# Two product forms in the feed-forwards' gate and up stage, and another order of the late projections in the first block

## What is computed

```python
t_mat = triangular_solve(a_mat, eye)     # 32 matrices of 64x64: the substitution
za, qb, zb, ga, gb = split(h @ w_rest)   # the late projections: 3584 columns

def _swiglu(h, w_gate, w_up, w_down):    # 4 times: 2 layers x 2
    return (jax.nn.silu(h @ w_gate) * (h @ w_up)) @ w_down
```

## Time and profile before

| | |
|---|---|
| Median of 3 runs | 1714.55 us (1713.25 to 1716.82) |
| The profiled execution | 1717.84 us, of it 1715.9 us span |
| TensorE busy | 1566.3 us, 91% of the span |
| VectorE busy | 978.8 us, 57% |
| ScalarE busy | 604.1 us, 35% |
| GpSimd busy | 205.0 us, 12% |
| Chain that ended last | PE 78%, DVE 10%, ACT 6%, DMA 2%, issue 2% |
| Gate and up products | 3 x 1408 matmuls of 256 columns |

### The profile page before, as it was taken

How to read it: one execution, slowest core, us unless ns; L and a number is a source line. 1 busy time by engine, 2 the same in 40 slices (tenths; PEclk the granted TensorE clock), 3 DMA queues, 4 the chain that set the end, 5 groups by cost and what they waited for, 6 DMA issues and landing times.

```text
span 1715.9 us, 21713 instructions
## 1 busy us (share of the span) xinstructions
PE 1566.3 (91%) x8944; PEld 1231.6 (72%) x8944; DVE 978.8 (57%) x1482; ACT 604.1 (35%) x945; POOL 205.0 (12%) x205
## 2 busy tenths in 40 slices
PE   7997869888889999899989998799998999989998
PEld 2646446545469997785459996699977865489986
DVE  0477775844147777355337776467776453275444
ACT  2425121132034443262234443444433531153442
POOL 0021142000001110043001110011100240001100
PEclk9998969998989999999989999999999999989999
DMA  9444323133347869332338887377976323457551
GB/s 343 141 128 146 98 75 123 59 126 122 123 146 264 282 229 359 130 123 92 106 111 269 265 288 276 116 247 257 311 281 217 123 74 111 147 178 227 185 172 49
DMA packets 192105, 305.44 MB, mean 178 GB/s; under 512 B 6139, under 2 KB 116487, under 8 KB 191879
## 3 DMA queue, kind: packets, MB, share of 16 engines
q1 hardware_dynamic: 189088, 299.45, 51.5%
q10 hardware_dynamic: 2919, 4.61, 0.7%
HBM read 302.99 MB, written 1.05 MB: 177 GB/s over the span
## 4 chain that ended last, share of the span: by engine, by line
PE 78%; DVE 10%; ACT 6%; DMA 2%; issue 2%; POOL 1%; ACTq 0%; DVEq 0%; POOLq 0%
PE ps L380 76%; DVE accs L521 2%; PE ps L383 2%; DVE wlo L1955 1%; ACT whi L1913 1%; DMA ring<-in_w_mod_dram 1%; DMA ring<-in_ffn_w_down_dram 1%; DVE arena L1212 1%; DVE arena L1209 1%; DVE H L1802 1%; DVE H L1736 1%; ACT arena L1447 0%; DVE misc L1514 0%; ACT hhi L1918 0%; DMA ctab<-in_consts_dram 0%
## 5 line engine op out<-in xcount | busy, mean ns | idle before, releaser
L1955 DVE TENSOR_TENSOR wlo<-ring,whi 128x1024 fp32r<-128x1024 f32 x264 | 322.5, 1225 | 221.9 <-ACT whi L1913 215.1
L380 PE MATMUL ps<-hhi,whi 128*128 128x256 f32 x1408 | 406.5, 289 | 20.9 <-DVE hlo L1961 14.9
L380 PE MATMUL ps<-hlo,whi 128*128 128x256 f32 x1408 | 402.0, 286 | 0.0
L380 PE MATMUL ps<-hhi,wlo 128*128 128x256 f32 x1408 | 401.9, 285 | 0.0
L1913 ACT ACTIVATE whi<-ring 128x1024 fp32r<-128x1024 f32 x264 | 274.8, 1055 | 314.4 <-PE ps L380 281.1
L380 PEld LDWEIGHTS ps<-hhi,whi 128*128 128x128 f32 x1408 | 274.4, 195 | 23.4 <-DVE hlo L1961 21.7
L380 PE MATMUL ps<-ring,H 128*128 128x512 f32 (+1 forms) x608 | 266.7, 589 | 13.5 <-ACT arena L1007 6.1
L380 PEld LDWEIGHTS ps<-hlo,whi 128*128 128x128 f32 x1408 | 274.2, 195 | 1.7 <-issue 1.7
L380 PEld LDWEIGHTS ps<-hhi,wlo 128*128 128x128 f32 x1408 | 274.0, 195 | 0.0
L380 PEld LDWEIGHTS ps<-ring,H 128*128 128x128 f32 x608 | 114.6, 195 | 134.1 <-issue 116.8
L521 DVE SCALAR_TENSOR_TENSOR accs<-ring,misc,accs 128x512 f32<-128x512 f32 x266 | 201.3, 757 | 2.7
(11 more groups left out here) (289 smaller groups left out, 1429.5 us busy)
## 6 DMA issues: line engine op xcount, KB each, us to landing
ring<-in_w_mod_dram SPq DMA_DIRECT2D x84, 1024.0 KB, 6.3
ring<-in_w_in_dram SPq DMA_DIRECT2D x48, 1024.0 KB, 5.1
ring<-in_ffn_w_gate_dram SPq DMA_DIRECT2D x44, 1024.0 KB, 7.3
ring<-in_ffn_w_up_dram SPq DMA_DIRECT2D x44, 1024.0 KB, 5.5
ring<-in_ffn_w_down_dram SPq DMA_DIRECT2D x44, 1024.0 KB, 6.5
ring<-in_w_out_dram SPq DMA_DIRECT2D x12, 1024.0 KB, 4.9
gates<-in_b_mod_dram SPq DMA_DIRECT2D x7, 512.0 KB, 7.3
ring<-in_w_proj_a_dram SPq DMA_DIRECT2D x2, 1024.0 KB, 6.1
```

The costliest lines, as they stand in the source:

```text
L380: return self.e.matmul(o, lhsT, rhs, start=start, stop=stop)
L1955: v.done(v.e.tensor_tensor(lo, M.slot(key)[:, r0:r0 + rn, :], plain(hi), ALU.subtract), ("split", l, sub, n), *([M.freed(key)] if ends els ...
```

## The change

In the feed-forwards HHI and HLO become the two halves of one tensor HH. The products hi x hi and hi x lo of a contraction tile become one product of 512 columns with `whi` as the stationary operand: columns 0 to 255 get hi x hi, columns 256 to 511 get hi x lo. The product lo x hi (256 columns) is added to the first half. Gate and up of a tile get a PSUM bank each; the pool `"ga"` now has six banks, so that a tile takes the two banks that the tile three before it held. The tail of a tile becomes longer: ScalarE copies the second halves of both banks (512 elements) into SG, VectorE adds the first halves of both (512 elements) and frees the banks, then ScalarE takes silu of the sum in SG (256), VectorE multiplies (256, both operands in SG), and `ahi` and `alo` follow as before. The copies, the sums, the silus and the products of the two tiles of a pair are each done for both before the next kind. TensorE reports the first tile of a pair when it is done, half a piece before the second. In `split_all` the tail now comes before the split of the pair's fourth piece is handed on, and not behind it. The column counts stay: 768 for each contraction tile and hidden tile, in two products and not three.

In the first block the order of the late projections is 1, 2, 0, 3, 4 and not 1, 2, 3, 4, 0. Before the wait for the substitution TensorE does 14 ticks of them and not 8 (tiles 1, 2, 0 and half of 3), and the tick behind y6 goes. Tile 0 uses banks 6 and 7. ScalarE takes tile 2 out before it waits for the substitution, and tile 0 after the first copies of y5. The weights of 1, 2, 0, 3 are fetched in a row, then two chunks of w_mod, then those of 4.

```diff
...
 NS = 5
-POOLS = {... "ga": (0, 1, 2, 3),
+POOLS = {... "ga": range(6),
          "down": (2, 3, 4, 5), "chain": (2, 3, 4, 5), "proj": (0, 1), "rec": (2, 3), "sd": (4, 5, 6), "dbo": (7,), "outx": (2, 3, 0, 1), "ds": (4, 5, 6, 7), "turnf": (6, 7, 0, 1), "turnx": (6, 7, 4, 5)}
...
         with nc.sbuf_tensor("arena", [128, self.AR], f32) as arena:
             self.arena = arena
         self.WHI, self.WLO = self.sbr("whi", [128, 4, 1024]), self.sbr("wlo", [128, 4, 1024])
-        self.HHI, self.HLO = self.sbr("hhi", [128, 8, 256]), self.sbr("hlo", [128, 8, 256])
+        self.HH = self.sbr("hh", [128, 2, 8, 256])
+        self.HHI, self.HLO = self.HH[:, 0, :, :], self.HH[:, 1, :, :]
         self.AHI, self.ALO = self.sbr("ahi", [128, 22, 256]), self.sbr("alo", [128, 22, 256])
         self.slots, self.banks, self.at = {}, {}, 0
         self.misc_at = self.bc_at = 0
...
 def pe_rest(pe, part):
     for n in part:
-        yield from pe_tok(pe, ("rest", n), 256, "rest")
+        yield from pe_tok(pe, ("rest", n), 256, "mods" if n == 0 else "rest")
 def act_rest(a, n, *after):
...
 def sp_delta(sp, mods):
-    run(sp_rest(sp, [1, 2]))
-    tick(mods, 8)
-    rest = sp_rest(sp, [3, 4, 0])
-    tick(rest, 1)
-    tick(mods, 8)
-    run(rest)
+    run(sp_rest(sp, [1, 2, 0, 3]))
+    tick(mods, 16)
+    run(sp_rest(sp, [4]))
 def pe_blocks(pe, key, col, pairs, width):
...
 def pe_delta(pe, mods):
     M = pe.M
-    fill = pe_rest(pe, [1, 2, 3, 4, 0])
+    fill = pe_rest(pe, [1, 2, 0, 3, 4])
     pe.sums = "mods"
     pe_tokens(pe, 1, M.VF, ("silu", 7))
     for blk in range(2):
...
         pe_decay(pe, n)
         if n in (5, 7):
             tick(fill, 1)
-    tick(fill, 6)
+    tick(fill, 12)
     lo, up = slice(0, 64), slice(64, 128)
     l5 = [(slice(0, 32), slice(32, 64)), (slice(64, 96), slice(96, 128))]
     B, F, G, Y5, Y6 = M.B, M.F, M.G, M.Y5, M.Y6
...
             pe.wait_ge(("x5 out", s, 0), ("x5 out", s, 1))
             pairs = [(at % 8, B[lo, m, up], (G[lo, m, :] if d == 0 else F[lo, m, lo])) for m, at in mats(s, d)]
             pe_blocks(pe, ("y6", s, d), 64, pairs, 64)
-    tick(fill, 1)
     for s in range(2):
         for d in range(2):
             pe.wait_ge(("y6 out", s, d))
...
     act_tokens(a, 1, M.VTOK)
     act_decays(a, 4, 10)
     act_rest(a, 1, ("dd read", 9), ("dd read", 7))
+    act_rest(a, 2)
     a.wait_ge(("tx",), ("clear",))
     for b in range(4):
         a.done(a.e.activation(blocks(M.F, b, 0, b), turned(M.TX, b, 0), ACT.Copy), ("blocks",))
-    act_rest(a, 2)
     for s in range(2):
         key = ("y5", s, 0)
         a.wait_ge(key)
         a.done(a.e.activation(M.Y5[32:64, s * 16:s * 16 + 16, :], M.ps(key)[32:64, :].rearrange("p (m c) -> p m c", c=32), ACT.Copy),
                ("y5 out", s, 0), ("free", key))
+    act_rest(a, 0, ("blocks",))
     for s in range(2):
         key, m0, m1 = ("x5", s, 0), slice(s * 16, s * 16 + 8), slice(s * 16 + 8, s * 16 + 16)
         a.wait_ge(key)
...
         a.wait_ge(key)
         a.done(a.e.activation(M.F[0:64, s * 16:s * 16 + 8, 64:128], M.ps(key)[0:64, :].rearrange("p (m c) -> p m c", c=64), ACT.Copy),
                ("x6 out", s), ("free", key))
-    for n in (3, 4, 0):
+    for n in (3, 4):
         act_rest(a, n, ("x6 out", 1), ("blocks",))
...
 def spare(M):
-    return [M.H[:, k, 256:512] for k in range(8)]
+    return [M.H[:, 2 * i:2 * i + 2, 256:512] for i in range(3)]
 def piece(M, i, n):
...
     ps_ = pieces(l, sub)
     for f in range(0, 22, 2):
         for q in range(4):
+            if q == 3:
+                yield f
             if f < 20:
                 emit(ps_[4 * (f // 2) + 4 + q])
             elif q < 3:
                 emit(ps_[44 + q])
             if work is not None:
                 tick(work, beside(f, q))
-        yield f
     emit(ps_[47])
     for kt in range(19):
         yield ("down", kt)
...
 def act_ffn(a, l, sub):
     M = a.M
-    SG = spare(M)[0:3]
+    SG = spare(M)
     def emit(p):
         n, key, r0, rn, wd_, _ = p
...
     for p in first[1:]:
         emit(p)
     for f in split_all(a, l, sub, emit, None):
-        for j in range(2 if isinstance(f, int) else 0):
-            i, key = (f + j) % 3, ("gu", l, sub, f + j)
-            a.wait_ge(("gu", l, sub, f), ("alo", l, sub, f + j - 3))
-            a.done(a.e.activation(SG[i], M.ps(key)[:, 0:256], ACT.Silu), ("silu", l, sub, f + j))
+        pair = range(f, f + 2) if isinstance(f, int) else ()
+        for x in pair:
+            key = ("gu", l, sub, x)
+            b = M.banks[key, 0]
+            a.wait_ge(key, ("alo", l, sub, x - 3))
+            a.done(a.e.activation(SG[x % 3], M.psum[:, b:b + 2, 256:512], ACT.Copy), ("copied", l, sub, x))
+        for x in pair:
+            a.wait_ge(("summed", l, sub, x))
+            a.done(a.e.activation(SG[x % 3][:, 0, :], SG[x % 3][:, 0, :], ACT.Silu), ("silu", l, sub, x))
+        for j, x in enumerate(pair):
+            i = x % 3
             a.wait_ge(("act", l, sub, f + j))
-            a.done(a.e.activation(M.AHI[:, f + j, :], SG[i], ACT.Copy), ("ahi", l, sub, f + j))
+            a.done(a.e.activation(M.AHI[:, f + j, :], SG[i][:, 0, :], ACT.Copy), ("ahi", l, sub, f + j))
 def pool_ffn(g, l, sub):
     M = g.M
-    SG = spare(M)[0:3]
+    SG = spare(M)
     for f in range(22):
         g.wait_ge(("ahi", l, sub, f))
-        g.op(g.e.tensor_tensor(M.ALO[:, f, :], SG[f % 3], plain(M.AHI[:, f, :]), ALU.subtract), ("alo", l, sub, f))
+        g.op(g.e.tensor_tensor(M.ALO[:, f, :], SG[f % 3][:, 0, :], plain(M.AHI[:, f, :]), ALU.subtract), ("alo", l, sub, f))
 def v_ffn(v, l, sub, work):
     M = v.M
-    SG = spare(M)[0:3]
+    SG = spare(M)
     def emit(p):
         n, key, r0, rn, wd_, ends = p
...
     for f in split_all(v, l, sub, emit, work):
         for j in range(2 if isinstance(f, int) else 0):
             i, key = (f + j) % 3, ("gu", l, sub, f + j)
+            b = M.banks[key, 0]
+            v.wait_ge(("copied", l, sub, f + j))
+            v.done(v.e.tensor_tensor(SG[i], SG[i], M.psum[:, b:b + 2, 0:256], ALU.add), ("summed", l, sub, f + j),
+                   ("free", (key, 0)), ("free", (key, 1)))
+        for j in range(2 if isinstance(f, int) else 0):
+            i = (f + j) % 3
             v.wait_ge(("silu", l, sub, f + j))
-            v.done(v.e.tensor_tensor(SG[i], SG[i], M.ps(key)[:, 256:512], ALU.mult), ("act", l, sub, f + j), ("free", key))
+            v.done(v.e.tensor_tensor(SG[i][:, 0, :], SG[i][:, 0, :], SG[i][:, 1, :], ALU.mult), ("act", l, sub, f + j))
 def pe_ffn(pe, l, sub, work):
     M = pe.M
     for f in range(0, 22, 2):
-        bs = [pe.bank(("gu", l, sub, f + j), "ga") for j in range(2)]
         for q in range(4):
             n = 2 * f + q
             hi, lo = piece(M, n, 256)
-            o0, k0 = 256 * (q // 2), 4 * (q % 2)
+            k0 = 4 * (q % 2)
             pe.wait_ge(("split", l, sub, n), ("hlo", l, sub, q % 2))
             for j in range(2):
-                c = slice(j * 128, j * 128 + 128)
-                for kt in range(4):
-                    ins = pe.mm3(bs[j][:, o0:o0 + 256], (hi[:, kt, c], lo[:, kt, c]), (M.HHI[:, k0 + kt, :], M.HLO[:, k0 + kt, :]),
-                                 k0 + kt == 0, k0 + kt == 7)
-            pe.done(ins, ("staged", l, sub, n), *([("gu", l, sub, f)] if q == 3 else []))
+                c, key = slice(j * 128, j * 128 + 128), ("gu", l, sub, f + j)
+                if q == 0:
+                    for i in range(2):
+                        pe.bank((key, i), "ga")
+                b = M.ps((key, q // 2))
+                for kt in range(k0, k0 + 4):
+                    low = lambda: pe.mm(b[:, 0:256], lo[:, kt - k0, c], M.HHI[:, kt, :], False, False)
+                    if kt:
+                        low()
+                    ins = pe.mm(b, hi[:, kt - k0, c], M.HH[:, :, kt, :], kt == 0, kt == 7)
+                    if kt == 0:
+                        low()
+                if q == 3 and j == 0:
+                    pe.done(ins, key)
+            pe.done(ins, ("staged", l, sub, n), *([key] if q == 3 else []))
             tick(work, beside(f, q))
     bs = [[pe.bank(("d", l, sub, blk, hf), "down") for hf in range(2)] for blk in range(2)]
     for k0 in range(19):
```

2 lines of the change are left out of this document (1 added, 1 removed).

## The result

| | before | changed |
|---|---|---|
| Median of 19 runs each | 1716.07 us (1712.61 to 1720.95) | 1706.57 us (1699.70 to 1715.10) |
| Ratio | | 0.9948, 95% interval 0.9935 to 0.9961 |
| The profiled execution, its span | 1717.84 us, 1715.9 us | 1711.62 us, 1709.6 us |

The change makes the kernel 8.9 us faster (0.0052 x 1716), not 26.7. The direction was right; the time lies above the forecast's range of 1672 to 1704.

What follows compares the result with a forecast made beforehand. TensorE sets the pace in gate and up, VectorE close behind; in the first block TensorE stands still for VectorE's substitution. Feed-forwards -11.7 and first block -15 make -26.7, from 1714.55 to 1687.8 us; range 1672 to 1704.

Steps and rivals of the forecast that it cites:

- The wide product: Gate and up stages: 0.347 us a contraction tile, not 0.360; 18.7 us less over four stages if TensorE alone decides.
- The tail: First three gate and up stages: VectorE's longer tail makes TensorE wait, leaving 2.5 us less per stage and not 4.7.
- the wait at its end: End of gate and up: the down stage waits for banks the last tiles hold, 1.6 to 2.2 us in first and third.
- VectorE is there about 3 us earlier: First and third down stages: VectorE's steps come about 3 us earlier, so the new bank wait ahead of them counts nothing.
- the ring: Weight slots: up's slot is freed 3 us later; 1 us added to each of the first three stages for a late slot.
- The fourth feed-forward: Last feed-forward, with modulation steps in its first four pairs only: 5.9 us less, 1.7 of it from the down-stage wait.
- The first block: Six more ticks fill TensorE's 21.1 us gap; the fence comes at 311 and not 326.6, -15 us, between -10 and -19.
- the wait at tile 4: First block, behind x6: TensorE waits for ScalarE to take tile 3 out of banks 0 and 1; 3.5 us lost.
- 128 records at the 0.0206 us that the warm ones of x5 take: First block, y5 behind the substitution: it finds a warm clock and takes 2.6 us, not 6.4.
- Everything behind the fence moves with it.: After the first block: the whole gain to the fence is kept, with 0 us change from there to the first feed-forward.
- The slower side: Gate and up: the tail lengthens VectorE's pair past TensorE's old pace, bank waits in each pair's first piece; 1755 us, chance 0.09.
- the wide product saves nothing: Gate and up: two runs of 256 columns cost as much as two products, pace stays 11.52 us; 1696.6 us, chance 0.09.

Runs made afterwards that it cites:

- ffn_only: The changed kernel with the first block's stage as before, so only the feed-forwards are changed; 1712.22 us, 0.9984 of the kernel before.
- delta_only: The kernel before with only the first block's new order of late projections, feed-forwards as before; 1711.26 us, 0.9977 of the kernel before.
- one_step: The changed kernel with one modulation step at every piece, never two; 1687.58 us, 0.9835 of the kernel before.
- before_one_step: The kernel before with one modulation step at every piece, never two; 1693.16 us, 0.9894 of the kernel before.
- one_step_banks: The changed kernel with one modulation step at every piece and tile 4 of the late projections in banks 6 and 7; 1680.73 us, 0.9811 of the kernel before.
- old_tail: The changed kernel with the tail moved back behind the split of the pair's fourth piece; 1837.7 us, 1.0730 of the kernel before.

## Why the prediction was wrong

By the medians of `ffn_only` and `delta_only` the feed-forwards gave 2.7 us of the 11.7 forecast and the first block 4.0 of 15. Both halves failed, by 9 and by 11 us.

**The wide product** (forecast 18.7 us in all, 0.347 us a contraction tile). Mis-sized: the runs show 0.352 and 0.360, which saves 1408 x 0.008 = 11 us. The step that failed read the extra of 0.0133 us off two streams of one width each, in two stages, and took it as a property of each product. The wide product of this stage has about 0.019 (0.232 less 0.2133), even in a row of its own width. Neither the layout nor the order of widths nor the load of the other engines explains the 0.005; what does stays open. Per product taken out, the saving is 8 ns by the timeline, 5.5 by the spans. The Trainium skill, "TensorE: Matmul & The Clock Gate", section "Back-to-back issue gap", has about 2.5 ns for the fixed part of an isolated warm product, by which an estimate for 1408 would be 3.5 us. The measurement lies between that and my 13.3, and it decides. The same section of the Trainium skill also says that the spacing in a stream is set by the load of the stationary operand and the product together, which speaks against adding up one width's spacing and another's as I did.

**The tail** (forecast 2.5 us less for a stage, the wait at its end apart). The mechanism is right: waits of 1.33 and 0.41 us for the sum, and one of 0.06, stand in the first piece of three pairs of the first stage, and the wait at its end is 2.38, forecast 1.6 to 2.2. They are fewer than forecast: two or three of ten pairs in each of the three stages, not most. Without the wait at its end the stage takes as long as before: 352 x 0.008 = 2.8 us less for products, 1.8 in these waits; the other 1.0 I did not trace. The forecast gave the products 1.9 us too much, and the tail 2.2 us of loss where it was 2.8. That tail and banks cost 5 us of the kernel even where VectorE is not late was not in the sum; one place of it is the fourth stage, where TensorE waits 3.2 us for the last chunk in `one_step` and 0.3 in `before_one_step`.

**"VectorE is there about 3 us earlier".** Wrong. VectorE makes the step that frees the slot at 142.5 us from the start of the stage, 142.2 before, as the double row of steps at 629.91 shows:

```profile
629.91 1.53 DVE L522 SCALAR_TENSOR_TENSOR accs<-ring,misc,accs 128x512 f32<-128x512 f32 x2
632.03 1.23 DVE L1962 TENSOR_TENSOR wlo<-ring,whi 128x1024 fp32r<-128x1024 f32 x1 [0.60 <-ACT whi L1913]
```

TensorE's waits in the first down stage say the same: 2.38 us at its start and 1.99 for VectorE's step 17 us later, where it was nothing and 4.10 before. So the new wait fell ahead of the old one, as forecast, but no time was gained. A gate and up stage cannot hand on time that the fourth down weight takes back, and I had priced the ring with 1 us for a late slot and not looked which piece frees the slot. `before_one_step` shows that the doubled steps cost 18 us in the kernel before as well. In the second feed-forward, the worst (+3.8, forecast -2.8), the wait at the down stage should have become 1.3 us shorter than the 3.48 of the earlier trace rows; it grew to 4.22, the products behind it ran at 1.2 GHz as they had behind the 3.48, and a later wait, for a step of VectorE in the down stage, is 3.33, where it was 1.90:

```profile
1025.50 0.66 PE L381 MATMUL ps<-whi,ahi 128*128 128x512 f32 x1 [4.22 <-DVE H L1985]
...
1055.62 1.34 PE L381 MATMUL ps<-accs,ctab 128*128 128x512 f32 x2 [3.33 <-DVE accs L522]
```

Together the first three came to +4.9 in this execution and to between -0.4 and -2.1 in the three others with the same feed-forwards, and not to -5.8.

**The fourth feed-forward** (forecast -5.9): -5.7, but in part by luck. Gate and up with the wait at its end gave 4.0 of the 5.9, since the products gave less. The other 1.6 came in the down stage: the wait at its start, where 2.15 us stood, is 0.25, and the products behind it are no longer at 1.2 GHz, where the forecast counted no change.

```profile
1642.50 0.50 PE L381 MATMUL ps<-whi,ahi 128*128 128x512 f32 x1 [0.25 <-DVE H L1985]
1642.84 0.40 PE L381 MATMUL ps<-wlo,ahi 128*128 128x512 f32 x1
```

**The first block** (forecast -15, bounds -10 and -19). -9.3 in the profiled pair; over the eight profiled kernels with the new first block and the banks as changed it is 87.5 to 88.8, over the three with the old one 94.9 to 96.8, some 7 us, and 4 in `delta_only`'s median. The gap was filled as forecast, and the wait at tile 4 came (2.43, forecast 3.5). Three steps failed. The first is "128 records at the 0.0206 us that the warm ones of x5 take". y5 did start at full clock, and in ten of the eleven profiled kernels with the new first block it ran at full clock to its end; it took 3.86 us there, 0.030 each, and not 2.6 (`one_step`, columns as in the earlier trace rows):

```profile
228.22:232.08 3.86, 3.86 (x128) 3.82 (x128) 3.75 (x4) 1.36 (x3) 3.86 (x5) 1.00 0.81 276
232.20:238.00 5.80, 5.80 (x15) 2.78 (x16) 4.57 (x6) 0.78 (x2) 5.80 (x5) 0.71 0.01 3
```

The second is that the clock would stay. TensorE had been busy at 1.00 until y5 began, but for 0.7 us, and 1.2 GHz comes behind y5: in `one_step` the tick takes 5.40 us, and the tick behind x5 again 5.40, where 3.43 were counted for each. In the changed kernel's own execution it came earlier: y5 took 4.71 us and its tick 6.09, and the tick behind x5 3.70. The short wait ahead of y5 is not enough to explain it: behind 1.33 us of waiting at 516.30, in the gate and up stage, the granted clock stays 1.00. x6 ended 26.7 us behind the substitution there and not 22.8. The third is the recurrence: the first tick behind the wait at tile 4 was slow too (5.37), and, with four ticks left, waits of 2.7 and 4.3 us stand there with a clock of 0.71 before the fence. I had named a falling clock and longer hand-offs as the bound of -10. Even that was too much: the profiled kernels together say 7.

**"Everything behind the fence moves with it."** Nearly: 160.6 to 160.9 us from the fence to the first feed-forward in these eight, 158.5 to 160.0 in the three. Up to 2 us are given back. The clock of the 6 us behind the fence doesn't explain it alone: it is 0.72 in the changed kernel and 0.73 before, 1.00 in `ffn_only` (158.5 us), but 0.51 in `one_step_banks`, which has the shortest stretch of all (157.9).

**The mixers** were in no sum. They take 176.2 to 176.4 us or 178.4 to 179.1, with one of 177.9. The first products behind a wait of the same length tell the two:

```profile
708.97 5.21 PE L380 MATMUL ps<-H,X 128*128 128x128 f32 x31 [2.83 <-DVE H L1751]
```

```profile
698.81 5.49 PE L381 MATMUL ps<-H,X 128*128 128x128 f32 x24 [2.83 <-DVE H L1749]
```

The first is the kernel before (granted clock of its 6 us 0.74), the second the changed kernel (0.50). Over the whole mixer it is 0.99 and 0.97; a second low stretch stands some 87 us into the longer form. The longer form stands in 17 of the 20 mixers of the ten profiled kernels with the new gate and up stage (`old_tail` not among them), in 1 of 6 of the others. `before_one_step` has one of each, so it doesn't need the change, and `old_tail`, which has the new stage, has the shorter form twice, so the change doesn't force it. The Trainium skill, "TensorE: Matmul & The Clock Gate", section "What's actually happening", says that the chip's activity window runs free of the kernel, by which the level would depend on the phase. No run here shows that. The levels fall more unevenly between the two groups than I can put down to chance, and why stays open. Up to 5 us of the change's cost may sit here.

**The rivals.** The slower side (bank waits in each pair) was right as a mechanism and needed `old_tail` to show at full size; "the wide product saves nothing" was too hard, 8 ns being left of 13.3. What happened is none of the cases alone: 60% of the products' gain, half of that lost to tail and banks, waits for VectorE's sums at the ends of the stages, the ring in the first three, and the first block at a quarter to a half of its 15 us (4.0 in the median, 7 to the fence).

## What to carry to other kernels

Before a stage is made faster, look at what the next stage's first inputs wait for: here a ring slot that was freed by a side job's step, and changing the count of those steps by six was worth twice the whole change. Spacing read in one stage is not that of the same width in another (0.227 us there, 0.232 to 0.235 here); take a difference from a run where only the form changes. Work moved into a gap is missing where it was: what is left is worth more when it is spread over the steps of a latency chain than in the first of them (3.4 us to the fence). Before a stage table of one execution is read, look whether that execution lies at the median.
